# Sparse-attention layer of a decoder step: who issues the index pages, and how the tail of the top-k search is ordered

## The reference, cut to what matters

```
q, k, v, qi, ki, wi = split_cols(xn @ w_in1)       # 8 query heads, 2 kv heads, 8 index heads of 64
logits = einsum('bqhd,bsd->bqhs', qi, ki_all) * 64**-0.5
score  = einsum('bqhs,bqh->bqs', relu(logits), wi * 8**-0.5)
score  = where(visible, score, -inf)
_, idx = top_k(score, 256)
o      = softmax(q . k[idx]) v[idx]                # then @ w_out1, residual, MLP
```

## Time and profile before

| | us |
|---|---|
| median of 3 timed runs | 2813.6 (2808.52 to 2816.48) |
| the profiled execution, its own time | 2809.43 |
| its span, first to last instruction | 2807.7 |
| `phase_in1` to `phase_topk`, within the span | 1324 to 1738 |
| mean granted TensorE clock, share of full | 0.951 |

### The profile page before, as it was taken

The page is one execution under the profiler, slowest core; times in us unless marked ns, Lnnn a source line. Parts: engine busy times, 40 slices in busy tenths (PEclk is TensorE's granted clock), DMA queues, the critical chain, the costliest instruction groups (busy, mean ns, idle before and its releaser), DMA issues. The chain is left out here.

```text
span 2807.7 us, 43411 instructions
## 1 busy us (share of the span) xinstructions
PE 2656.1 (95%) x16469; PEld 2540.1 (90%) x16469; DVE 1097.1 (39%) x2395; ACT 567.1 (20%) x1011; POOL 1189.0 (42%) x1520
## 2 busy tenths in 40 slices
PE   7999879999999999999878998999999999999998
PEld 7899758999999999999747997788999999999998
DVE  6959365342112121123258974655332121121223
ACT  3010143221010010111034533444121010010112
POOL 5534303555455555556302411000655455554552
PEclk8999978999999999999879986999999999999998
DMA  6534443311111111111212224202111111111111
GB/s 200 107 79 95 113 136 94 110 38 45 48 49 46 45 45 45 47 51 42 89 29 83 85 74 143 84 16 76 45 38 48 50 45 45 45 45 49 48 45 68
DMA packets 291412, 188.45 MB, mean 67 GB/s; under 512 B 41030, under 2 KB 281290, under 8 KB 290522
## 3 DMA queue, kind: packets, MB, share of 16 engines
q1 hardware_dynamic: 271350, 179.85, 21.3%
q10 hardware_dynamic: 19940, 7.01, 2.1%
HBM read 151.84 MB, written 34.98 MB: 67 GB/s over the span
## 5 line engine op out<-in xcount | busy, mean ns | idle before, releaser
L403 POOL TENSOR_TENSOR w_hi<-w_raw,ones 128x256 fp32r<-128x256 f32 x720 | 620.0, 892 | 1321.9 <-PE ps L414 1194.6
L406 POOL TENSOR_TENSOR w_lo<-w_raw,w_hi 128x256 fp32r<-128x256 f32 x720 | 527.7, 764 | 25.6
L414 PE MATMUL ps<-next_hi,w_hi 128*128 128x344 f32 x1920 | 417.9, 327 | 13.5 <-PEq L1902 9.0
L414 PE MATMUL ps<-out_x_hi,w_hi 128*128 128x344 f32 x1920 | 408.5, 321 | 6.9 <-DVE out_x_lo L1939 6.9
L414 PE MATMUL ps<-next_lo,w_hi 128*128 128x344 f32 x1920 | 412.9, 324 | 0.0
L414 PE MATMUL ps<-next_hi,w_lo 128*128 128x344 f32 x1920 | 410.5, 323 | 0.0
L414 PE MATMUL ps<-out_x_lo,w_hi 128*128 128x344 f32 x1920 | 408.2, 321 | 0.0
L414 PE MATMUL ps<-out_x_hi,w_lo 128*128 128x344 f32 x1920 | 406.3, 320 | 0.0
L1964 DVE TENSOR_TENSOR resid<-ps,resid 128x344 f32 (+1 forms) x240 | 108.9, 509 | 705.3 <-PE ps L414 705.3
L414 PEld LDWEIGHTS ps<-next_hi,w_hi 128*128 128x128 f32 x1920 | 327.2, 191 | 15.2 <-issue 14.3
L414 PEld LDWEIGHTS ps<-out_x_hi,w_hi 128*128 128x128 f32 x1920 | 324.1, 188 | 7.3 <-issue 7.3
(11 more groups left out here) (551 smaller groups left out, 2783.7 us busy)
## 6 DMA issues: line engine op xcount, KB each, us to landing
w_raw<-in_w_up SPq DMA_DIRECT2D x64, 512.0 KB, 4.1
w_raw<-in_w_down SPq DMA_DIRECT2D x64, 512.0 KB, 4.0
w_raw<-in_w_in SPq DMA_DIRECT2D x36, 512.0 KB, 4.4
resid_spill<-resid SPq DMA_DIRECT2D x2, 4128.0 KB, 13.7
ml_inputs<-in_ring SPq DMA_DIRECT2D x16, 516.0 KB, 2.8
resid<-resid_spill SPq DMA_DIRECT2D x4, 2064.0 KB, 7.7
w_raw<-in_w_out SPq DMA_DIRECT2D x16, 512.0 KB, 4.2
keys<-in_cache_k SPq DMA_DIRECT2D x64, 128.0 KB, 2.0
```

Source lines behind the costliest of these rows:

```text
L403: m.nc.gpsimd.tensor_tensor(parts(hi[:, k]), x[:, k], one, ALU.mult)
L406: last = m.nc.gpsimd.tensor_tensor(parts(lo[:, k]), x[:, k], hi[:, k], ALU.subtract)
L414: ins = nc.tensor.matmul(out[c], parts(w), parts(x[:, token_cols(c)]), start=first and n == 0, stop=last and n == 2)
```

## The change

It has three parts.

1. Index pages. The page table is loaded by SP at the start of `phase_in1`. ScalarE, after its square root there, issues the 40 page loads of samples 0 to 4; SP issues the other 24 in `phase_index`. All eight samples have tiles of their own: six in the part of `keys` that `phase_in1` doesn't use, two in the part that it does. `rect` gets four tiles instead of two, `gap` becomes 4. The sample scores move from behind step 47 to step 40 (VectorE) and 44 (TensorE).
2. `phase_topk`. Six k-steps instead of three run before search step 0. Tasks begin at step 21. From task 11 on the transposes alternate between banks 3, 4 and banks 0, 1, and from task 12 on `turn_keys(t)` stands ahead of `key_logits(t - 1)`. Unit 10 is evicted ahead of all sets, set 0 comes first instead of third, two k-steps of unit 11 stand ahead of the page counts, and its eviction stands before set 4 instead of set 6.
3. The weight splits of the first two `w_out1` units move from `phase_topk` to `phase_attend`, on GpSimd.

```diff
@@ l1_tiles
-    s.rect = [c.take(1024) for _ in range(2)]
-    s.pages = [c.take(PAGES, IDIM) for _ in range(4)]
+    s.rect = [c.take(1024) for _ in range(4)]
+    at = 2 * N + KT * (IDIM + IH)
+    late = Carver(m.keys[:, :, 0:at])
+    early = Carver(m.keys[:, :, at:])
+    s.pages = [t.take(PAGES, IDIM) for t in (early,) * 6 + (late,) * 2]
@@ phase_in1, sync
+            sp.dma_start(s.table, m.ins["page_table"].rearrange("(a b) j -> a (b j)", a=1)).then_inc(m.dma_b.sem, 16)
@@ phase_in1, scalar
             last_tile_act(act, m, m.g_mix[1])
+            act.wait_ge(m.dma_b.sem, m.dma_b.at(16))
+            for b in range(5):
+                for j in range(PAGES):
+                    page = act.value_load(s.table[0:1, b * PAGES + j:b * PAGES + j + 1], min_val=0, max_val=last_page)
+                    act.dma_start(s.pages[b][:, j], m.ins["cache_kidx"][bass.ds(page, 1)].rearrange("a p d -> p (a d)")
+                                  ).then_inc(m.page_in[b].sem, 16)
@@ phase_index
-    first, gap = 3, 5
+    first, gap = 3, 4
+    sum_at, turn_at = 40, 44
-            for b in range(B):
-                if b >= 4:
-                    sp.wait_ge(m.pe_c.sem, m.pe_c.at(b - 3))
+            for b in range(5, B):
@@ phase_topk
-            return range(3 * step + 3, min(3 * step + 6, KT * Q_UNITS))
+            return range(3 * step + 6, min(3 * step + 9, KT * Q_UNITS))
@@ phase_topk, gpsimd
-            for u in range(2, units + 2):
+            for u in range(2, units):
@@ phase_topk, tensor
             next_keys()
+            for k in range(2):
+                unit_step(KT * (units - 1) + k)
             pe.wait_ge(m.dve_b.sem, m.dve_b.at(BITS + 2))
...
-            for k in range(KT):
+            for k in range(2, KT):
                 unit_step(KT * (units - 1) + k)
-            for _ in range(2):
-                t += 1
-                next_keys()
             pe.wait_ge(m.dve_e.sem, m.dve_e.at(1))
...
+            t += 1
+            next_keys()
             while t < 2 * B - 1:
                 t += 1
-                next_keys()
+                turn_keys(t)
+                key_logits(t - 1)
@@ phase_topk, vector
+            for u in range(max(ended.values()) + 1, units - 1):
+                evict(u)
             V.drain()
-            for i, x, n in sets[1:3] + sets[0:1] + sets[3:]:
+            for i, x, n in sets:
                 w = x.shape[1]
-                if i == 0:
-                    for u in range(max(ended.values()) + 1, units - 1):
-                        evict(u)
-                if i == 6:
+                if i == 4:
                     evict(units - 1)
@@ phase_attend
+        @block.gpsimd
+        def _(pool):
+            for slot in range(2):
+                split_unit(pool, m, slot, 0)
```

More of the change, by code:

```diff
@@ L2277, in phase_in1 @@
     place_in(m, 1)
+    s = l1_tiles(m)
+    last_page = m.ins["cache_kidx"].shape[0] - 1
     with nc.Block() as block:
@@ L2339, in phase_rows @@
     m.left.close()
[L2340 removed]
+    s = m.l1
     x = m.proj
@@ L2419, in phase_index @@
     last_page = m.ins["cache_kidx"].shape[0] - 1
-    first, gap = 3, 5
+    first, gap = 3, 4
+    sum_at, turn_at = 40, 44
+    n_rect = len(rect)
     with nc.Block() as block:
@@ L2492, in _ @@
                     e = min(w, c + 512)
-                    last = nc.scalar.activation(rect[n % 2][:, c:e], m.ps[2 * (n % 3) + c // 512][:, 0:e - c], ACT.Relu)
+                    last = nc.scalar.activation(rect[n % n_rect][:, c:e], m.ps[2 * (n % 3) + c // 512][:, 0:e - c], ACT.Relu)
                 last.then_inc(m.act_a.sem, 1)
@@ L2544, in _ @@
                     keep_keys((n - first) // gap)
[L2545 to L2552, removed]
+                if n == sum_at:
+                    token_scores()
             dve.wait_ge(m.pe_b.sem, m.pe_b.at(2))
@@ L2621, in unit_steps @@
     def unit_steps(step):
+        if step < 0:
+            return range(0, 6)
         if step < first_turn - 1:
-            return range(3 * step + 3, min(3 * step + 6, KT * Q_UNITS))
+            return range(3 * step + 6, min(3 * step + 9, KT * Q_UNITS))
         return range(KT * Q_UNITS + 2 * (step - first_turn + 1), KT * Q_UNITS + 2 * (step - first_turn + 2))
@@ L2698, in turn_keys @@
                     pe.wait_ge(m.page_in[b].sem, m.page_in[b].at(16 * PAGES))
+                if t == two_from + 1:
+                    pe.wait_ge(m.set_free.sem, m.set_free.at(units + 2))
                 if t >= 1:
[L2700 removed]
+                    pe.wait_ge(m.act_b.sem, m.act_b.at(t if t <= two_from else t - 1))
                 for j in range(PAGES):
[L2702 removed]
+                    last = nc.tensor.transpose(turned_of(t)[j // 4][:, (j % 4) * PAGE:(j % 4 + 1) * PAGE],
                                                k_pages[b % 2][:, j, g * DH:(g + 1) * DH], m.ident[:])
@@ L2777, in copy_keys @@
                 for half in range(2):
-                    last = nc.scalar.copy(keys_t[t % 2][:, 4 * half:4 * half + 4].rearrange("p j k -> p (j k)"), turned[half][:])
+                    last = nc.scalar.copy(keys_t[t % 2][:, 4 * half:4 * half + 4].rearrange("p j k -> p (j k)"), turned_of(t)[half][:])
                 last.then_inc(m.act_b.sem, 1)
```

39 lines of the change are left out of this document (23 added, 16 removed).

## The result

The changed kernel takes **2779.95 us** (median of 4 runs, 2777.62 to 2784.59) against 2811.06 for the kernel before (4 runs): a ratio of 0.9888, 95% interval 0.9873 to 0.9903, so 31 us or 1.1% faster. The prediction was 2770, in a range of 2752 to 2787. The profiled execution took 2777.73, with a span of 2776.0.

What follows compares the result with a forecast made beforehand. TensorE was taken as the bound, busy 95% of the span, with the index phase waiting for SP's page issues. Terms +2 - 22 + 0 - 22 + 0.5 = -41.5 gave 2772 on the median, stated as 2770, range 2752 to 2787.

Steps and rivals of the forecast that it cites:

- ScalarE's issues, +2: End of phase_in1: 40 page issues on ScalarE at 1.09 us each make the barrier come 2 us later.
- The rival with dearer issues: Before the barrier: ScalarE's issues at 1.5 us each, barrier 18.6 us late, kernel at 2787; chance 12%.
- the one that ended slower: Before the barrier: 40 issues at 2.12 us or more each make the kernel slower than before; chance 2%.
- Index phase, -22: Index phase: page waits go, leaving mainly TensorE's own work; 93 to 71 us, -22.
- 22.6 (1420): Index phase: TensorE's higher clock taken from about 1420 on, with the page waits gone.
- my 25, 30 to 31 and 16: Index phase terms: steps 0 to 15, 25 us; blocks 4 to 6, 30 to 31; block 7, 13, plus 3 of lag.
- the rival "stays at 1.2 GHz": Index phase: clock stays at 1.2 GHz, gaining 11 us instead of 22, kernel at 2781; chance 15%.
- Search, 0: Search: +1.3 inside the steps, offset by about as much low clock saved before step 0; 0, bounds -1.5 to +3.
- Tail, -22: After the search: unit 11 starts earlier and fewer tasks remain behind it; -22 us, bounds -15 to -29.
- The events of the list: Tail: unit 10 evicted first, VectorE's hidden 3 us wait, a 3 to 5 us key-page wait, then 1.2 GHz.
- Splits in attention, +0.5: Start of phase_attend: GpSimd's weight splits slow VectorE's small operations by sharing; +0.5 us of a bound of 2.
- the 30% that I took from the earlier trace: Attention: bound on sharing cost for a VectorE operation between SBUF tiles, 1.60 us beside a GpSimd split, 1.23 alone.

Runs made afterwards that it cites:

- before_again: The kernel before, unchanged, run and profiled once more; 2813.81 us, ratio 1.0004.
- before_third: The kernel before, unchanged, run and profiled yet another time; 2812.10 us, ratio 1.0003.
- topk_only: The kernel before with only the top-k and attention phases as changed, index phase as before; 2793.38 us, ratio 0.9940.
- index_only: The changed kernel with the top-k and attention phases of before, so only the index part changed; 2794.59 us, ratio 0.9949.
- after_again: The changed kernel, unedited, run and profiled once more; 2776.30 us, ratio 0.9876.
- first22: The changed kernel with key tasks starting at search step 22 instead of 21; 2780.74 us, ratio 0.9891.
- interleave: The changed kernel with one k-step moved between logits and transposition in each search step with a task; 2784.99 us, ratio 0.9905.
- old_search: The changed kernel with the search steps of before: 3 k-steps ahead of step 0, first key task in step 22; 2782.72 us, ratio 0.9906.
- ahead4: The changed kernel with 4 k-steps ahead of search step 0 instead of 6; 2777.84 us, ratio 0.9884.
- turn11: The changed kernel with key task 11 transposed ahead of the last six k-steps instead of behind them; 2784.45 us, ratio 0.9900.
- act48: The changed kernel with 48 index pages on ScalarE's queue and 16 on SP's; 2787.16 us, ratio 0.9924.
- best: The changed kernel with 4 k-steps ahead of step 0, task 11 transposed earlier, 32 index pages per queue, weight splits back in top-k; 2781.95 us, ratio 0.9885.

## Why the prediction was right, point by point

Here are the same stages in all fourteen traces (us). Half clock is the number of 8 us stretches at 0.50 (up to 0.53) from the start of the index phase, "to step 0" runs from that start, "long" are the search steps of 7.3 us and more behind step 0. The first step with a key task isn't among them: it is shorter, and took 4.1 us in seven traces and 5.6, a fall too, in the other seven.

```
trace         root to  half   to      search  long  tail   rest
              barrier  clock  step 0
before          42.6    4    106.40   149.84   2    84.46  1069.6
before_again    42.6    4    106.85   156.03   5    84.22  1070.0
before_third    42.6    5    105.08   156.10   5    84.32  1070.0
topk_only       42.6    5    106.96   157.60   5    63.14  1070.8
index_only      43.8    2     89.11   150.66   2    84.53  1069.9
after           44.1    1     84.28   157.59   5    64.13  1070.8
after_again     43.9    2     89.73   155.49   4    64.98  1070.1
first22         43.9    4     99.08   154.06   4    68.86  1072.5
interleave      43.8    3     92.91   158.12   5    64.07  1073.1
old_search      43.3    2     86.01   154.00   4    70.29  1070.8
ahead4          44.1    1     84.08   155.07   4    63.15  1070.8
turn11          43.9    4     99.10   157.64   5    61.96  1072.5
act48           52.1    2     87.12   154.55   4    63.83  1070.8
best            42.5    3     99.38   154.97   4    60.25  1070.2
```

- **ScalarE's issues, +2: right.** The barrier moved by 1.3 us on average; an issue costs 1.07, where 1.09 was taken from SP's row. The rival with dearer issues is out, and so is the one that ended slower.
- **Index phase, -22: the mechanism right, the size met by luck.** The page waits are gone in every trace with the new pages. But the 71 us, which the first trace met at 70.6, came with a clock that rose after 9 us, not the 22.6 (1420) that I counted. `interleave` rose after 24, near my assumption, and its phase took 79.4. By the parts of the working (steps 0 to 15; blocks 4 to 6; block 7 with the lag):

```profile
1396.60:1424.40 27.80, 27.43 (x76) 14.21 (x76) 13.17 (x29) 8.07 (x16) 0.29 (x1) 0.56 0.13 29
1424.40:1459.00 34.60, 34.60 (x154) 20.29 (x154) 23.31 (x27) 18.25 (x46) 0.88 (x3) 0.90 0.01 1
1459.00:1476.00 17.00, 9.68 (x35) 4.30 (x31) 15.59 (x16) 9.80 (x20) 1.15 (x2) 0.89 0.00 0
```

They are 27.8, 34.6 and 17.0 for my 25, 30 to 31 and 16: each term was too small, 8 us in all, and the early rise of the first trace hid it. Over the eight traces with the 40/24 pages, step 0 comes 90.5 us after the start (84.1 to 99.1), against 106.3 over the four with the old ones: **-15.8**. The table orders them by the clock: one stretch of half clock 84, two 86 to 90, three 93, four 99. That part of the rival "stays at 1.2 GHz" was real, not as one case against the other but as a spread of 15 us from one execution to the next. Closing gaps does not cure it: `first22` has none behind its first 8 us.
- **Search, 0: the step that was mis-sized, by less than the first trace says.** Over five traces each with the old steps and the changed ones the means are 153.3 and 156.6, **+3.3**, with 3.6 and 4.6 long steps of 1.55 us extra each. +1.3 was in the working (a key task more, a k-step less); the lower clock that work ahead of step 0 would save did show, 6.18 to 4.64 in step 0. What the working left out is that it comes back: TensorE then waits 1.5 us more for VectorE ahead of steps 20 and 21, as the pair `first22` and `old_search` shows. With full clock in all key steps the first two traces would have searches of 146.7 and 148.2 (an estimate: 2 and 6 falls of 1.56 us taken off), so +1.5 stands without the clock. And I had no term for the low clock in the key steps. Counting the first step with a key task too, it hits 20 of 40 in the old order and 27 of 45 in the changed one, and one key step more brings one more to hit. Whether the order does more than that, ten traces that scatter from 149.8 to 157.6 do not tell.
- **Tail, -22: right, -20.5** (84.4 over four traces, 63.9 over the six with the changed tail and first key task in step 21). The events of the list are in the trace: unit 10 evicted ahead of the sets, VectorE's hidden wait of 3.7, the new wait for key pages of 4.33, half clock behind it. `turn11` shows what that wait was worth on the path: 2 us, since the clock fell sooner without it.
- **Splits in attention, +0.5: right in sign, the size not settled.** The rest takes 1070.1 to 1073.1 with them and 1069.6 to 1070.2 without, +1.4 on average. By the source lines, three of VectorE's first operations there, all between SBUF tiles, can grow: in the changed kernel's first trace a 64x64 one from 0.25 us to 0.80, the 128x512 one from 0.69 (L3143 before) to 1.23 (L3169 now), and the 128x64 one behind it from 0.22 to 0.74. They don't grow each time. In `after_again` and `first22` the 128x512 one took 0.69 as before, yet the rest was 1070.1 in the one and 1072.5 in the other; so these operations, 0.8 to 1.6 us in all, aren't what made three traces longer than 1072, and what did is open. That an operation grows by up to 0.55 us or not at all, depending on when it starts, and at most by nearly a whole GpSimd piece of 0.7, is what the Trainium skill says of this pair of ports ("SBUF — State Buffer", on the shared pair as an exclusive lock: the loser waits for the whole instruction). The trace agrees with it here better than with the 30% that I took from the earlier trace rows. GpSimd's pieces grow as well: the one beside the end of the 128x512 operation (1714.61 to 1715.83) and the 128x64 one behind it took 1.17 us where the piece before it took 0.73.

```profile
1714.56 0.73 POOL L406 TENSOR_TENSOR w_lo<-w_raw,w_hi 128x256 fp32r<-128x256 f32 x1
1715.24 1.17 POOL L406 TENSOR_TENSOR w_lo<-w_raw,w_hi 128x256 fp32r<-128x256 f32 x1
```

The means add up to +1.3 - 15.8 + 3.3 - 20.5 + 1.4 = -30.3, beside the measured -31. Against the predicted -41.5 the index phase makes 6 of the 11 that are missing, the search 3, tail and attention 2.5; the barrier gave 0.7 back. The gain was three quarters of the forecast one. The 4 runs of `after_again` bring the changed kernel's median over eight to 2777.7.

The queue was the point on which page and rows disagreed. The Trainium skill ("DMA: Bandwidth & Descriptors", section "Issuing engines are not separate DMA queues") has a second issuing engine save only the sequencer's time, usually little. Here that time was what the phase waited for: one issue with its page from a register took 1.07 to 1.09 us, 64 of them in a row 69.84 of the phase's 93.0, and `index_only`, which moved 40 of them, gained 14 to 17 us. How much of that is the queue alone, and how much the new tiles and places that came with it, was not measured.

## What to carry to other kernels

Where small transfers with computed addresses stand in a row, count issues times the duration of one before looking at bytes; if that chain is the bound, another engine's idle queue can be worth what TensorE then doesn't wait, and every issue beyond that engine's slack is paid in full (8 more of them moved the barrier by 8.0 us). A wait that is taken away uncovers the clock: what was free behind it (half speed in a phase that waited anyway) becomes the new bound, with its scatter. Work that is moved ahead of a stage to fill idle time there is worth nothing if the stage has light steps in which another engine sets the pace. And a sum that is met to 0.4 us can be wrong in its terms: compare the terms with a trace that has the condition they assumed. Where the clock moves within a stage, a term that is read from one trace can be off by 6 to 15 us, and a second and third trace of the unchanged kernel are the cheapest experiment there is.

## What the runs showed of the hardware that I had not expected

- TensorE at half its clock for 9, 16, 24 or 34 us from the start of the same code, without a gap in its work (26.00 busy of 26.00 in `first22`), from one execution to the next. It was at half clock already when the phase began: the row shows the changed kernel's 8 us ahead of it, with TensorE idle. What decides when it rises is not known from these runs.

```profile
1391.10:1399.10 8.00, 0.00 (x0) 0.00 (x0) 1.87 (x10) 0.00 (x0) 7.19 (x16) 0.50 0.15 33
```

- In the search, key steps of 5.85 and of 7.4 us alternate or follow each other, with TensorE busy throughout (54.50 of 54.50 us in the changed kernel), in a pattern that can differ between executions of one kernel: 2, 5 and 5 long ones in the three of the kernel before.
- While the index phase waited for pages, its length did not follow the clock: four traces with 32 to 41 us at half clock all reach step 0 within 105.1 to 107.0 (the lowest, 105.08, with 41).
